# Delta-rule block: all four head groups projected first with paced background work, the gate projection last, and the output projection begun before the last heads

## The reference

```python
proj = h @ w_in                                   # 1024 -> q, k (8 heads), v, z (16 heads), gates
qkv  = silu(causal_depthwise_conv(proj[..., :o1], conv_w))      # convolution of 4 taps
z    = proj[..., o1:o2]
beta = sigmoid(proj[..., o2:o3]);  g = -exp(a_log) * softplus(proj[..., o3:] + dt_bias)
# per value head and chunk: a_mat = I + (beta k k^T) * decay * strictly lower triangle
sol  = triangular_solve(a_mat, [beta v, beta k exp(G)])          # u, w
# recurrence over the chunks, with a state S of 128 x 128 per head:
v_new = u - w S;   o = (q exp(G)) S + attn v_new;   S = S exp(G_last) + kt^T v_new
out  = (rms_norm(o, norm_w) * silu(z)) @ w_out                   # 2048 -> 1024
hs   = hs + rms_norm(out, norm_w2)
```

## Time and profile before

| | |
|---|---|
| median of 3 runs | 1678.58 us |
| profiled execution, whole | 1676.21 us |
| profiled execution, its span | 1674.1 us |
| mean granted TensorE clock | 0.942 |
| weights and other data read | 222.91 MB |
| delta-rule layer's tasks from block 42 to the last z block | 51.0 to 375.7 us of the span |
| output projection | 382.2 to 439.8 us |

### The profile page before, as it was taken

How to read it: one execution, slowest core, us unless ns; L and a number is a source line. 1 busy time by engine, 2 the same in 40 slices (tenths; PEclk the granted TensorE clock), 3 DMA queues, 4 the chain that set the end, 5 groups by cost and what they waited for, 6 DMA issues and landing times.

```text
span 1674.1 us, 35078 instructions
## 1 busy us (share of the span) xinstructions
PE 1597.6 (95%) x14211; PEld 1496.7 (89%) x14211; DVE 1112.6 (66%) x2282; ACT 946.5 (57%) x2003; POOL 344.0 (21%) x405
## 2 busy tenths in 40 slices
PE   6998999998999999999899999999999999999998
PEld 5987987798889999896789999898999998899998
DVE  3876686566588864664769984766766656676664
ACT  6753564456256654454547664546676554567754
POOL 3331222233033322000303430200301210031010
PEclk9997896999799999898779999999999999999999
DMA  4420221134265554342236675544445555454452
GB/s 166 150 78 3 82 85 51 40 114 138 78 201 176 175 171 148 102 150 88 88 101 195 190 217 183 188 152 150 149 130 164 182 197 164 149 167 132 153 170 89
DMA packets 64977, 230.41 MB, mean 138 GB/s; under 512 B 7313, under 2 KB 9489, under 8 KB 64817
## 3 DMA queue, kind: packets, MB, share of 16 engines
q1 hardware_dynamic: 59792, 217.67, 41.6%
q0 software_dynamic: 4160, 8.98, 1.8%
q10 hardware_dynamic: 864, 1.52, 0.3%
HBM read 222.91 MB, written 5.24 MB: 136 GB/s over the span
## 4 chain that ended last, share of the span: by engine, by line
PE 78%; DVE 12%; ACT 5%; issue 3%; DMA 1%; POOL 1%; ACTq 0%; SPq 0%; DVEq 0%; POOLq 0%
PE ps L602 76%; DVE splitL L2210 4%; DVE arena L2218 2%; PE ps L606 2%; ACT splitH L1630 1%; DVE mixT L2215 1%; ACT arena L1635 1%; DVE arena L2215 1%; ACT L1635 1%; ACT arenaR L1635 1%; ACT sq L1635 1%; DVE arena L2226 1%; DMA ring<-wst 1%; POOL sq L3007 0%; DVE rst L2230 0%
## 5 line engine op out<-in xcount | busy, mean ns | idle before, releaser
L2210 DVE TENSOR_TENSOR splitL<-ring,splitH 128x512 fp32r<-128x512 f32 x767 | 564.1, 764 | 235.0 <-ACT splitH L1630 225.8
L602 PE MATMUL ps<-aH,splitH 128*128 128x272 f32 (+2 forms) x2232 | 662.5, 298 | 14.8 <-ACT aH L1635 8.2
L602 PE MATMUL ps<-aH,splitL 128*128 128x272 f32 (+2 forms) x2232 | 640.9, 288 | 0.0
L602 PE MATMUL ps<-aL,splitH 128*128 128x272 f32 (+2 forms) x2232 | 626.4, 286 | 0.0
L1630 ACT ACTIVATE splitH<-ring 128x512 fp32r<-128x512 f32 x824 | 479.7, 622 | 126.1 <-PE ps L602 116.0
L602 PEld LDWEIGHTS ps<-aH,splitH 128*128 128x128 f32 x2232 | 429.7, 193 | 35.6 <-issue 21.2
L602 PEld LDWEIGHTS ps<-aH,splitL 128*128 128x128 f32 x2232 | 430.0, 193 | 0.0
L602 PEld LDWEIGHTS ps<-aL,splitH 128*128 128x128 f32 x2232 | 420.4, 191 | 0.4
L602 PE MATMUL ps<-arenaR,splitH 128*128 128x256 f32 (+2 forms) x1856 | 353.8, 291 | 9.7 <-DVE arenaR L2215 8.0
L602 PEld LDWEIGHTS ps<-arenaR,splitH 128*128 128x128 f32 x1856 | 295.2, 193 | 12.5 <-issue 8.4
L602 PE MATMUL ps<-arenaR,splitL 128*128 128x256 f32 (+2 forms) x928 | 266.7, 287 | 0.0
(11 more groups left out here) (195 smaller groups left out, 1283.9 us busy)
## 6 DMA issues: line engine op xcount, KB each, us to landing
ring<-wst SPq DMA_DIRECT2D x412, 512.0 KB, 3.8
mem_scratch<-arenaR POOLq DMA_DIRECT2D x16, 128.0 KB, 4.3
arenaR<-mem_scratch POOLq DMA_DIRECT2D x4, 512.0 KB, 7.8
rel_scratch<-arena POOLq DMA_DIRECT2D x8, 255.5 KB, 4.5
arena<-x SPq DMA_DIRECT2D x2, 512.0 KB, 5.3
arena<-mem POOLq DMA_DIRECT2D x2, 512.0 KB, 4.4
arena<-rel_scratch POOLq DMA_DIRECT2D x1, 1024.0 KB, 9.3
out<-arena ACTq DMA_DIRECT2D x4, 256.0 KB, 2.0
```

What stands on the lines that cost most here:

```text
L602: return pe.matmul(out, lhsT, rhs, start=start, stop=stop)
L2210: dve.tensor_tensor(lo, raw, hi.bitcast(F32), ALU.subtract).then_inc(*inc(("lo_dve", q)))
```

## The change

The change has five parts.

1. `hsT` is copied to DRAM (`hscr`) by a DMA from POOL before the layer and read back by another in `core(3)`, once the last group has done with its buffers. In between its space holds q, k and v of group 3. So every group has its own `qkT`, and phase 3 no longer waits for group 0.
2. z gets other buffers, and the product of z and o is a background task (`zmul`) instead of a part of the main one. The inverse's small buffers are laid out so that the low parts `oL` have room.
3. The four projection phases are paced. Their main turns yield `"pace"`: after each, background tasks get only 0.7 of the time that main took, instead of everything that is due. In z all that is due runs, as before. `core(g)` starts as soon as q and k of the group are projected, instead of after v.
4. The output projection starts with three tiles at once: blocks 0 to 11 of tiles 0, 1 and 2 (heads 0 to 11), then blocks 12 to 15 of the three (heads 12 to 15). `oH` and `oL` of the last heads are made between, `oL` of them on POOL.
5. `core` waits for the gates itself.

```diff
+PACE = 0.7
...
-    main = ("main",)
+    main, since, credit = ("main",), 0.0, 0.0
...
-        if v != "go":
+        if v == "pace":
+            credit += PACE * (pe.at - since)
+            while credit > 0:
+                at = pe.at
+                if not one(True):
+                    credit = 0.0
+                credit -= pe.at - at
+        elif v != "go":
             while one(True):
                 pass
+        since = pe.at
...
-        qkT = [al(4, T) for _ in range(3)]
-        vTs = [al(4, T) for _ in range(2)]
-        zT = [qkT[1], vTs[0], vTs[0], qkT[1]]
+        qkT = [al(4, T) for _ in range(3)] + [hsT[:, 0:4, :]]
+        vTs = [al(4, T) for _ in range(2)] + [hsT[:, 4:8, :]]
+        vT = [vTs[n] for n in (0, 1, 0, 2)]
+        zT = [qkT[0], vTs[1], vTs[0], vTs[1]]
+        Z_FREE = [[("qs", 0, 2)], [("vtr", 1, 2)], [("vtr", 2, 2)], [("zg", 1), ("zgp", 1)]]
+        Z_AFTER = [("vuse", 0, 2), ("vtr", 1, 2), ("vtr", 2, 2), ("zmul", 1)]
...
+        def in_turn(K, lead=0, first=0):
+            for part in (range(first), range(first, K)) if lead else ():
+                yield from ((m, k) for m in range(lead) for k in part)
+            yield from ((m, k) for m in range(lead, KD) for k in range(K))
...
                 for ph, tiles in enumerate(GDN_TILES):
-                    if ph == 3:
-                        yield from until("vuse", 0, 2)
...
-                                if kind == 2 and ph >= 2:
-                                    yield from until("vtr", ph - 2, 2)
-                                if kind == 3:
-                                    if x == 0:
-                                        yield from until("vuse", 1, 2)
-                                    if x == 4:
-                                        yield from until("vtr", 2, 2)
+                                if kind == 2 and ph == 2:
+                                    yield from until("vtr", 0, 2)
+                                if kind == 3 and x % 4 == 0:
+                                    yield from until(*Z_AFTER[x // 4])
+                                if m % 4 == 3:
+                                    late.append((kind, x // 4 if kind == 3 else m))
-                            yield
+                            yield "pace" if kind < 3 else None
...
+                    if (m, k) == (0, 12):
+                        for c in range(3):
+                            yield from until("out", 3, c)
...
+                if g == 3:
+                    w.wait_ge("kk", 3, 0)
+                    w.wait_ge("qs", 3, 2)
+                    w.wait_ge("vtr", 3, 2)
+                    pool.dma_start(hsT[:, :, :], hscr).then_inc(*inc(("hsr",), by=16))
...
+                pool.dma_start(hscr, hsT[:, :, :]).then_inc(*inc(("hst",), by=16))
                 yield from gdn()
-                yield from mix_sums("gdn", 16, T)
+                yield from mix_sums("gdn", 16, T, 3, 12)
```

More of the change, by code:

```diff
@@ L444, in build @@
         W = [dict(zip(("E", "Lt", "T", "Ca", "Cb"), small)) | {"At": small[5:7], "Tt": small[7:9]}]
[L445 to L449, removed]
+        W += [{"E": four(sqf[:, 512 * c - 512:512 * c]), "Lt": [], "At": [], "Tt": []} for c in (1, 2)]
+        TR = [None, [], []]
+        even = top[0]
+        for _ in range(2):
+            for c in (1, 2):
+                for n in ("Lt", "At", "Tt"):
+                    W[c][n].append(al(4, 128))
+                TR[c].append({n: al(4, 32) for n in ("M", "T", "Tt")} | {"T64": al(4, 64)})
         flat = mixT[:, :, :].rearrange("p a b -> p (a b)")
@@ L886, in core @@
                 spawn(("vtr", g))
+                yield from until("gates")
                 for part in PARTS:
@@ L1117, in out, with zmul @@
                 done.add(("out", g, c))
+            def zmul(g):
+                for c in range(3):
+                    yield from until("out", g, c)
+                yield 0.3
+                done.add(("zmul", g))
             def gdn():
@@ L1138, in flush @@
                     def flush():
-                        for gz in late:
-                            if gz == 3:
+                        for kind, n in late:
+                            if kind < 3:
+                                if n == 3:
+                                    spawn(("core", ph))
+                                else:
+                                    done.add(("v", ph))
+                            elif n == 3:
                                 done.add(("zs3",))
                             else:
-                                for c in range(3):
-                                    yield from until("out", gz, c)
+                                spawn(("zmul", n))
                         late.clear()
@@ L1163, in gdn, with gdn_out @@
                     for _ in d:
                         pass
-                    yield from flush()
+                    flush()
                     yield "go"
[L1167 to L1172, removed]
+                for g in range(3):
+                    yield from until("zmul", g)
+            def gdn_out():
+                bs = [fg.get("gdn", m) for m in range(3)]
+                for m, k in in_turn(16, 3, 12):
+                    if m >= 3:
+                        break
+                    if (m, k) == (0, 12):
+                        for c in range(3):
+                            yield from until("out", 3, c)
+                    h, l, end = take(128, ("gdn_w_out", 0, k * 128, 128 * m, 128))
+                    w.wait_ge("oL" if k < 12 else "oLp", k // 4)
+                    t = mm3(psum[bs[m]][:, 0:T], h, l, (oH[k // 4][:, k % 4, :], oL[k // 4][:, k % 4, :]), k == 0, k == 15)
+                    signal(t, end, *([("tile", "gdn", m)] if k == 15 else []))
+                    if k == 15:
+                        fg.put(bs[m], ("nsc", "gdn", m))
+                    yield
@@ L1677, in lead, with mix_sums @@
                     yield
[L1679 to L1687, removed]
[L1688 to L1690 removed]
+            def mix_sums(name, K, n, gi, lead=0, first=0):
+                if not first:
+                    dummy()
+                for m, k in in_turn(K, lead, first):
+                    if lead and (m, k) == (0, first):
+                        for c in range(3):
+                            w.wait_ge("oT3", 3, c)
+                        a(oH[3], oT[:, 12:16, :], ACT.Copy).then_inc(*inc(("oH", 3)))
+                        dummy()
+                    feed.take(128)
+                    if k == K - 1:
+                        b = ps(name, m)[:, 0:n]
+                        w.wait_ge("tile", name, m)
+                        a(sq[:, m, 0:n], b, ACT.Square).then_inc(*inc(("nsq", name, m)))
+                        a(mixT[:, m, 0:n], b, ACT.Copy, scale=V("norm_w", gi + m)).then_inc(*inc(("nmx", name, m)))
+                        a(sc[:, m, 0:n], b, ACT.Square, scale=V("norm_w", gi + m)).then_inc(*inc(("nsc", name, m)))
+                    yield
             def mix_out(name, K, n, gi):
@@ L2573, in out, with zmul @@
                         ALU.mult).then_inc(*inc(("oT3", g, c)))
+            def zmul(g):
+                w.wait_ge("zs", g)
+                for c in range(3):
+                    w.wait_ge("oT", g, c)
+                o_ = oT[:, 4 * g + 0:4 * g + 2, :]
+                tt(o_, o_, zT[g][:, 0:2, :], ALU.mult).then_inc(*inc(("zg", g)))
+                yield
             def gdn():
@@ L3109, in tri, with zmul @@
                     yield
+            def zmul(g):
+                w.wait_ge("zs", g)
+                for c in range(3):
+                    w.wait_ge("oT", g, c)
+                o_ = oT[:, 4 * g + 2:4 * g + 4, :]
+                tt(o_, o_, zT[g][:, 2:4, :], ALU.mult).then_inc(*inc(("zgp", g)))
+                yield
             def gdn():
```

162 lines of the change are left out of this document (62 added, 100 removed).

## The result

The changed kernel takes 1695.8 us (median of four runs, 1690.17 to 1698.37) against 1677.05 us before: ratio 1.0105, 95% interval 1.0066 to 1.0144. It is slower by about 18 us. The forecast was no change, 1676 us in a range up to 1692, so the time lies outside. The profiled execution took 1695.8 us, its span is 1694.0 us, 19.9 more than before.

A forecast was written before the change was run, and what follows sets the result against it. Bound: PE's blocks plus background turns, priced by what stands beside them. Layer 127.9 + 126.3 + 67.2 = 321.4 us against 324.7: 3.3 saved less 0.6, so 1673.5 profiled, 1676 us predicted; range 1653 to 1692.

The forecast's parts named there:

- mixed turn: A background turn in a stretch with projection blocks between the turns: 0.41 us each, 164 of them, 67.2 us.
- The bare turns: Background turns in stretches where they have PE to themselves: 0.554 us each, 228 of them, 126.3 us.
- The last block of z: Sign at the end of z: at about 372 us if right, before 355 or after 385 us if wrong.
- The second rival: Projections of groups 2 and 3: DVE and ACT become the bound, 0.47 us a mixed turn, 1689.5 us; chance 0.22.
- The first rival: Beside blocks a turn costs only PE's own share, 0.28 us: 21 us more saved, 1655 us; chance 0.28.
- Saving 0: Seam between z and output projection: the same chain stands before the first early block, so the early start saves 0.
- ACT reaches it when PE is about a unit in: Output projection: ACT reaches the last heads' `oH` about 3 us in, so 6 us are spare; cost 0.
- The table load: Before the silu in the seam: at best done during z, at worst 1.28 us longer; 0.6 us taken.
- The copies: `hsT` to DRAM and back: cost taken 0; 3.6 us each if DMA or POOL delayed PE in full.

The follow-up runs named there:

- the pace by tiles: The changed kernel with the same pace of 0.7, paid out after each tile of eight blocks instead of after each block: 1674.8 us, ratio to before 0.9985.
- the kernel with spread matmuls: The kernel before, with 16 unread 32 x 32 matmuls added after each of the 128 blocks of the delta-rule layer's output projection: 1831.9 us.

## Why the prediction was wrong

- **The step that failed: the price of a mixed turn.** The prediction took 0.41 us, the mean of the old mixed stretches, for all 164 mixed turns. For the 111 in the projections it was 0.58: 111 x 0.17 = 18.9 us. By the starts in the traces, the passages cost 0.11 us a turn in the old mixed stretches (38 passages for 120 turns) and 0.19 in the paced one (73 for 111), and the small matmuls themselves 0.27 and 0.34. So about half of the 0.17 is the passages, and nearly as much is that the turns were bigger: without the three rows of each block, PE has 13 rows a turn there (2104 - 636 over 111) and had 5.6 in the old mixed stretches. A mean over small turns was applied to large ones. With the pace by tiles the passages cost 0.06 us a turn and the price is still 0.51.
- **What the coarse grain gives back is the passages.** Of the 21.0 us by which the layer gets shorter, they are 17.8.
- **The old prices could not have shown it.** They are not in the order of passages: the stretch with most of them for its turns (8 for 17, from 229 to 254.2 us) was the cheapest, 0.28, because its small matmuls cost only 0.13 us a turn; the dearest, 0.47, had 13 for 35, and 0.34 us a turn. The prediction divided by turns and counted neither passages nor rows.
- **The bare turns held.** 0.56 to 0.59 against 0.554. The rest of the layer came out 3.5 us better than the sum had it (18.9 less the 15.4 by which 336.8 is over 321.4). The last block of z came at 387.8 us, beyond the 385 that the prediction names as a sign of being wrong.
- **The second rival was the right side by the wrong cause.** It allowed 0.47 us a mixed turn and blamed DVE and ACT. The coarse pace made DVE busier and the kernel faster.
- **The first rival** (a turn beside blocks costs PE's share alone) failed although its clock came: PE's clock was 0.95 in the stretch, and the turn was dear all the same. The rule that the prediction cites beside it from the Trainium skill (TensorE: Matmul & The Clock Gate, Part 1), that activity releases the slow clock, agrees with this 0.95; it does not agree with the kernel with spread matmuls, whose clock was 0.50 with PE busy throughout, and there the measurement decides.
- **The early start.** "Saving 0" held for the changed kernel: with the old order the seam is as long. Its cost did not: "ACT reaches it when PE is about a unit in" was wrong. ACT cannot run further ahead of PE than the buffers of the split weights let it, and nine halves stood before `oH`, so the ninth came when PE had almost done. Cost 5.9 us instead of 0.
- **The table load.** Taken at 0.6 us, it cost its full 1.3, the worst that the prediction named.
- **The copies.** No loss shows: the first 51 us are as long as before (block 42 at 49.7 us, before at 49.6), and the experiments with the old output order have the read back and its old length.

The sum: 18.9 (mixed turns in the projections) - 3.5 (rest of the layer) + 0.7 (table load) + 5.7 (output projection) = 21.8 us, of the 22.3 by which the profiled execution missed the 1673.5 us forecast.

## What to carry to other kernels

In this kernel, filling the waits of dependent small matmuls with large ones paid only where PE did not change between the two at every step; background work in lumps after 1.5 to 3 us of large matmuls (four to eight blocks) gave 21 to 24 us over a finer order. When pricing moved work by a mean over old stretches, count how often it is entered and how much of it there is in a turn. And an instruction put behind prefetching work on an in-order queue runs when the prefetch's buffers come free, which here was when PE was nearly there.

## What the hardware showed that was not expected

- PE's clock fell to 1.2 GHz (granted 0.50 over 40 us) with PE busy all the time, when 16 small matmuls stood after each block of three large ones. With the same work in lumps of 128 it was 0.87. A second price of mixing finely, then. In the changed kernel it hardly shows: 0.95 over the paced stretch, against 0.97 with the pace by tiles.
- What a passage costs depends on what comes next: 0.22 us to a first matmul on 16, 32 or 64 partitions, 0.13 to one of 128 partitions and at least 128 columns.
- A lump of 256 rows of 32 x 32 matmuls stops for about 2 us, with no wait in the trace (31.8 us in 16 lumps). The cause is open.
- The same order ran at different clocks. The changed kernel's first bare run took 22.3 us at 0.92, and in the kernel with the old output order, whose instructions there stand in the same sequence, 27.8 us at 0.69:

```profile
194.30:222.10 27.80, 23.50 (x216) 19.98 (x214) 13.69 (x43) 11.77 (x32) 0.62 (x2) 0.69 0.04 14
```

What decides between the two was not tried. In the same two kernels the run of 72 turns took 40.9 us at 0.83 and 44.1 at 0.77. So a difference of a few us in a stretch of small matmuls between two of these kernels can be the clock's alone.
